# Scores of the third attention: four heads in one run on TensorE, then their four turnings and value products

## The chip, the cores and the metric

The kernel runs on one core of a Trainium2 chip. The metric is the device time of one execution in microseconds (us). The engines are TensorE (PE; its weight loads are listed as PEld), VectorE (DVE), ScalarE (ACT), GpSimd (POOL) and SyncE (SP). Each has its own queue and runs it in the order written; semaphores tie the queues together. Matmul results go to PSUM, which is used as eight banks of 128 x 512 float32.

## The reference, cut to what matters

The program is two blocks in a row. The first is a hybrid layer, run twice (`l` = 0, 1), over 256 "context" rows and 256 "latent" rows, in tiles of 128 rows (tiles 0 and 1 are context, 2 and 3 latent). Each layer has three attentions and a merge. The third attention has 16 query heads of size 64 that share 4 key heads, a window mask and a sink:

```
s_loc = where(mask, q * 64**-0.5 @ kb.T, NEG_INF)
s_ctx = q * 64**-0.5 @ k_ctx.T
p     = softmax(concat([sink, s_ctx, s_loc]))     # float32
o     = p_ctx @ v_ctx + p_loc @ vb
```

Context rows attend to the 256 context rows alone. In layer 0 all four tiles have queries, in layer 1 only the two latent ones. The second block (four mixers) is not touched by the change.

## The kernel before, in words

The four engines' programs are generated by one list of steps. A linear layer is a step "gemm": weights come in by DMA in chunks of 256 rows, ScalarE makes a high part of them (L1265), VectorE the rest (L1774), and TensorE multiplies three times (L872 to L874). `prepare` issues that splitting; inside the third attention it comes once in a layer, on ScalarE ahead of item 32 (layer 0) or 16 (layer 1), on VectorE two items later.

An attention is a list of items, one for each (tile, head). The third has 64 items in layer 0 (0 to 31 on context tiles, with 256 keys; 32 to 63 on latent tiles, with 512 keys) and 32 in layer 1 (all latent). For each item:

- TensorE makes the scores. The head size is 64, so the array of 128 rows is used as two halves of 64 rows, and two heads are made side by side, each in a bank of its own: three steps (L1034, L1037, L1040; high by high, low by high, high by low) of two matmuls each. They are issued at even items only.
- VectorE adds the mask and takes the negative maximum in one instruction, in place in the bank (L2250).
- ScalarE takes the exponential out of the bank into `stage` (L1590), which frees the bank, and the sink's exponential (L1596).
- TensorE turns the probabilities (`turn`, L914, one 128 x 128 transpose per key tile), with item i - 3 (`LAG`).
- VectorE (even items, L2268) or ScalarE (odd items, L1609) copies them to `probs_turned`.
- TensorE multiplies them with the values (L1061), with item i - 5 (`PV_LAG`).
- VectorE scales the output of four heads (L2297, L2299, L2313). It does so after the maximum of item i = 4n + 2, for the group of items that ends with 4n - 1.

The order on VectorE is therefore, for i = 4n to 4n + 3: maximum; maximum, copy; maximum, outputs; maximum, copy. On ScalarE it is exponential and, at every other item, a copy behind it.

Banks: `take` hands out banks in turn from a pool and makes TensorE wait until the last user of the bank has emptied it. Scores use the pool "wide" (banks 0 to 3), the turnings banks 4 and 5, the outputs 6 and 7. Items 0 and 1 are scored earlier, inside the linear layer before, in other banks. So four items' scores fill the pool, and the scores of item i need the banks of item i - 4.

Below, S(i) stands for the scores of items i and i + 1, T(i) for the turning and V(i) for the value product of item i.

Of the kernel before, what the change touches and what calls it, by code (L numbers as in the profile page):

```python
# [28 lines left out]
P = 128  # L29
# [29 lines left out]
FIRST = 2  # L59
# [318 lines left out]
def key_tiles(t):  # L378

    return CTX_TILES if t in CTX_TILES else ALL_TILES  # L380
# [11 lines left out]
def program(nc, dram, out, known):  # L392
    ctx = ExitStack()
    with ctx:
# [7 lines left out]
        def place(name, shape, dt=F32, at=None):  # L402
            size = 4 * int(np.prod(shape[1:]))
            where = top[0] if at is None else at
            if at is None:
                top[0] += (size + 31) // 32 * 32
            return nc.alloc_sbuf_tensor_at(name, shape, dt, offset=where)
# [20 lines left out]
        QH = place("q_high", [P, 8, 512], F32R, at=R)  # L428
        KH = place("k_high", [P, 8, 512], F32R, at=R + K16)
# [78 lines left out]
        banks = [ctx.enter_context(nc.psum_tensor(f"bank{b}", [P, 512], F32)) for b in range(8)]  # L508
# [11 lines left out]
        def probs_at(r, i):  # L520

            return stage(i) if r == 1 else STG[:, 512 * ((i + 4) % 6):512 * ((i + 4) % 6) + 512]
# [7 lines left out]
        def q_low(l, r, h, n, t):  # L530

            if l:
                return QL_LAT[:, h:h + n, P * (t - 2):P * (t - 2) + P]
            return (QL_ACC if r == 1 else QL_X)[:, h:h + n, P * t:P * t + P]

        def k_low(l, r, h, n, cols):

            if r == 2:
                return KL_K[:, h:h + n, cols]
            if l == 0:  # L540
                return KL_X[:, h:h + n, cols]
            return KL_Y[:, h:h + n, cols] if h < 4 else KL_ACC[:, h - 4:h - 4 + n, cols]
# [13 lines left out]

        part_of = {c: n for n, c in enumerate(to_split)}
        summed = {sums.at[m] for u in units for _, sums, m in u.riders}
        first = len(FIRST_LANDING)
        landed_in = list(FIRST_LANDING) + [(c - first) % RAW_SLOTS for c in range(first, len(chunks))]  # L560
# [82 lines left out]
        def items(l, r, qt):  # L643
            return [(t, h) for t in qt for h in range(HEADS[r])]
# [150 lines left out]
        def _(pe):  # L795
# [7 lines left out]
            def take(pool, key):  # L803

                b = POOL[pool][turns[pool] % len(POOL[pool])]
                turns[pool] += 1
                if uses[b]:
                    pe.wait_ge(*S.nth(f"bank{b}_emptied", uses[b]))
                uses[b] += 1
                S.use_bank(key, b, uses[b])  # L810
                return b

            def fills(b):
                return S.up(f"bank{b}_filled")

            def once(event):

                sem, value = event
                if (str(sem), value) not in waited:
                    waited.add((str(sem), value))  # L820
                    pe.wait_ge(sem, value)
# [6 lines left out]
            def gemm(u, turned):  # L828
# [15 lines left out]
                for n, (src, k0, kt, col, width) in enumerate(u.chunks):  # L844
                    while late and late[0][0] <= n:
                        turn(*late.pop(0)[1])
                    if u.more.get("head") and n == 1:
                        l, r, qt = u.more["head"]
                        attend(l, r, qt, 0, FIRST)
# [57 lines left out]
            def turn(key, parts, pool="turn", after=()):  # L907

                for event in after:
                    once(S.at(*event))  # L910
                b = take(pool, key)
                for src, col in parts:
                    p, m = src.shape
                    mm = pe.transpose(banks[b][0:m, col:col + p], src, IDENT[0:p, 0:p])  # L914
                mm.then_inc(*fills(b))
# [81 lines left out]
            def qk_ready(l, r, t, h):  # L997

                q, k = {0: (("uq", l, h // 4), ("ukv", l, h // 2)), 1: (("dq", l, h // 4), ("dk", l, h // 4)),
                        2: (("sq", l, h // 8), ("sk", l))}[r]  # L1000
                once(S.emptied(("turn", q, t)))
                for kt in key_tiles(t):
                    once(S.emptied(("turn", k, kt)))

            def values_ready(l, r, t, h):

                for kt in key_tiles(t):
                    once(S.emptied(({0: ("ukv", l, h // 2), 1: ("dv", l, h // 4), 2: ("sv", l)}[r], kt)))

            def attend_first(l, r, qt):  # L1010
                pass

            def attend(l, r, qt, start=FIRST, stop=None):
                todo = items(l, r, qt)
                width = VALUE[r]
                for i in range(start, stop or len(todo)):
                    if i < len(todo):
                        t, h = todo[i]
                        nk = P * len(key_tiles(t))
                        qk_ready(l, r, t, h)  # L1020
                        if r == 0:
                            b = take("turn4" if i < FIRST else "wide", ("s", l, r, t, h, 0))
                            pe.matmul(banks[b][:, 0:nk], QT[0:MQ, h, P * t:P * t + P], KTT[0:MQ, h, 0:nk],  # L1023
                                      start=True, stop=True).then_inc(*fills(b))
                        elif r == 1 or h % 2 == 0:
                            halves = [(h, 0), (h, 1)] if r == 1 else [(h, 0), (h + 1, 0)]
                            two = [take("turn4" if i < FIRST else "wide", ("s", l, r, t, hh, m)) for hh, m in halves]
                            hq, hk = (h, h) if r == 1 else (h // 2, h // 4)
                            q_high, k_high = QH[:, hq, P * t:P * t + P], KH[:, hk, 0:nk]
                            ql = q_low(l, r, hq, 1, t).rearrange("p a c -> p (a c)")  # L1030
                            kl = k_low(l, r, hk, 1, slice(0, nk)).rearrange("p a c -> p (a c)")
                            for m, b in enumerate(two):
                                a = slice(64 * m, 64 * m + 64)
                                pe.matmul(banks[b][:, 0:nk], q_high[a], k_high[a], start=True, stop=False)  # L1034
                            for m, b in enumerate(two):
                                a = slice(64 * m, 64 * m + 64)
                                pe.matmul(banks[b][:, 0:nk], ql[a], k_high[a], start=False, stop=False)  # L1037
                            for m, b in enumerate(two):
                                a = slice(64 * m, 64 * m + 64)
                                pe.matmul(banks[b][:, 0:nk], q_high[a], kl[a], start=False,  # L1040
                                          stop=True).then_inc(*fills(b))
                    if LAG <= i < len(todo) + LAG:
                        t, h = todo[i - LAG]
                        pe.wait_ge(*S.at("probs", (l, r, t, h)))
                        pr = probs_at(r, i - LAG)
                        turn(("pt", l, r, t, h), [(pr[:, P * n:P * n + P], P * n) for n in range(len(key_tiles(t)))])
                    if i >= PV_LAG:
                        n_item = i - PV_LAG
                        t, h = todo[n_item]
                        g, gn = h // GROUP[r], h % GROUP[r]  # L1050
                        if gn == 0:
                            out_bank[0] = take("out", ("o", l, r, t, g))
                        open_bank = out_bank[0]
                        values_ready(l, r, t, h)
                        pe.wait_ge(*S.emptied(("pt", l, r, t, h)))
                        vcol = h * width if r < 2 else (h // 8) * width
                        kts = key_tiles(t)
                        slot = n_item % PT_SLOTS
                        pt = PTS[:, 512 * slot:512 * slot + 512]
                        for n, kt in enumerate(kts):  # L1060
                            mm = pe.matmul(banks[open_bank][:, width * gn:width * gn + width],  # L1061
                                           pt[:, P * n:P * n + P], V[:, kt, vcol:vcol + width],
                                           start=(n == 0), stop=(n == len(kts) - 1))
                        if gn == GROUP[r] - 1:
                            mm.then_inc(*fills(open_bank))
                            S.same("pt_used", (l, r, n_item), f"bank{open_bank}_filled")
                        else:
                            mm.then_inc(*S.up("pt_used", (l, r, n_item)))
# [1500 lines left out]
```

## Time and profile before

| | |
|---|---|
| time, median of 3 runs | 2450.35 us (2450.02 to 2450.39) |
| the profiled execution: its time | 2452.31 us |
| its span (first to last instruction) | 2450.5 us |
| granted TensorE clock, mean | 0.998 of full speed |
| busy share of the span | PE 98%, PEld 82%, DVE 60%, ACT 49%, POOL 1% |
| third attention, layer 0 | from 726.01 us (S(2)) to 812.02 us (first matmul of the next linear layer) |
| third attention, layer 1 | from 1444.85 us to 1497.58 us |

A row of a timeline gives the start, the duration, the engine, the source line, the operation, what it writes and reads, how many instructions are merged, and in brackets how long the engine sat idle before it and what released it. Matmuls are pipelined: the difference between the starts of two rows is the time that the first costs the engine, and its duration also holds the time until its result is out. A value product of 128 x 128 float32 counts as two instructions.

### The profile page before, as it was taken

To read this page: it belongs to the slowest core of one execution; us is meant where nothing else is said; L and a number is where in the kernel's file an instruction comes from. 1 tells how busy PE (TensorE), PEld (TensorE's weight loads), DVE (VectorE), ACT (ScalarE), POOL (GpSimd) and SP (SyncE) were. 2 spreads that over 40 slices of the span, in tenths; PEclk is the share of its full clock that TensorE was granted. 3 is DMA by queue.
4 is the path that set the end of the run, shared out by engine and by line. 5 is a ranking of instruction groups with operands and counts; after the bars stand their busy time and mean duration, and the time that the engine had idled before them with its cause. 6 is when DMAs were issued, how large, how long until landed. Compare 5 with 4: busy or idle time off the path is not lost.

```text
span 2450.5 us, 33381 instructions
## 1 busy us (share of the span) xinstructions
PE 2401.6 (98%) x12741; PEld 2009.1 (82%) x12741; DVE 1474.1 (60%) x2518; ACT 1190.1 (49%) x2278; POOL 29.9 (1%) x55
## 2 busy tenths in 40 slices
PE   7999999899999999899999999999999999999999
PEld 5978888678888888788887888878888888888887
DVE  3555564876557445565548676665679844566565
ACT  5553223653247332564336455464556554544643
POOL 1100000000000000000000000000000000000000
PEclk9999999999999999999999999999999999999999
DMA  7413553134530222234531623555555561655654
GB/s 253 104 30 104 167 150 86 44 100 133 157 93 10 87 86 78 69 117 130 146 94 41 193 87 92 193 172 185 161 190 185 185 189 40 217 174 163 197 168 133
DMA packets 165007, 318.80 MB, mean 130 GB/s; under 512 B 10470, under 2 KB 22624, under 8 KB 164336
## 3 DMA queue, kind: packets, MB, share of 16 engines
q1 hardware_dynamic: 161552, 303.67, 40.0%
q0 software_dynamic: 3296, 12.98, 1.9%
q8 instruction: 103, 1.69, 0.3%
q14 instruction: 56, 0.46, 0.1%
HBM read 313.46 MB, written 3.15 MB: 129 GB/s over the span
## 4 chain that ended last, share of the span: by engine, by line
PE 90%; DVE 6%; ACT 2%; issue 2%; DMA 0%; SPq 0%; DVEq 0%; ACTq 0%
PE bank L872 24%; PE bank L874 24%; PE bank L873 24%; PE bank L914 7%; PE bank L1061 5%; PE bank L1023 1%; DVE neg_max L2255 1%; DVE w_low_part L1774 1%; PE bank L1034 1%; PE bank L1189 1%; PE bank L1122 1%; PE bank L1148 0%; PE bank L1040 0%; PE bank L946 0%; PE bank L1037 0%
## 5 line engine op out<-in xcount | busy, mean ns | idle before, releaser
L1774 DVE TENSOR_TENSOR w_low_part<-w_raw,w_high_part 128x1024 fp32r<-128x1024 f32 (+3 forms) x544 | 636.8, 1186 | 510.8 <-ACT w_high_part L1265 508.7
L1265 ACT ACTIVATE w_high_part<-w_raw 128x1024 fp32r<-128x1024 f32 (+3 forms) x544 | 552.3, 1031 | 688.5 <-PE bank L874 688.3
L872 PE MATMUL bank<-w_high_part,h_high 128*128 128x512 f32 (+3 forms) x2128 | 817.1, 384 | 5.9 <-DVE w_low_part L1774 2.1
L874 PE MATMUL bank<-w_high_part,h_low 128*128 128x512 f32 (+3 forms) x2128 | 806.9, 379 | 0.0
L873 PE MATMUL bank<-w_low_part,h_high 128*128 128x512 f32 (+3 forms) x2128 | 806.0, 379 | 0.0
L872 PEld LDWEIGHTS bank<-w_high_part,h_high 128*128 128x128 f32 x2128 | 400.1, 188 | 83.5 <-DVE w_low_part L1774 6.0
L874 PEld LDWEIGHTS bank<-w_high_part,h_low 128*128 128x128 f32 x2128 | 399.9, 188 | 74.7
L873 PEld LDWEIGHTS bank<-w_low_part,h_high 128*128 128x128 f32 x2128 | 400.4, 188 | 71.3 <-issue 0.2
L1590 ACT ACTIVATE stage<-bank,neg_max 128x512 f32<-128x512 f32 (+1 forms) x240 | 147.1, 615 | 123.9 <-DVE neg_max L2255 71.1
L1061 PE MATMUL bank<-v,probs_turned 128*128 128x128 f32 x1280 | 173.9, 276 | 0.0
L914 PEld LDWEIGHTS bank<-ident,stage 128*128 128x128 f32 (+1 forms) x1112 | 127.3, 139 | 51.7 <-issue 38.6
L914 PE MATMUL bank<-ident,stage 128*128 128x128 f32 (+1 forms) x1112 | 167.3, 278 | 2.0 <-ACT probs_turned L1715 0.9
L1061 PEld LDWEIGHTS bank<-v,probs_turned 128*128 128x128 f32 x1280 | 158.6, 192 | 0.5
L872 PE MATMUL bank<-w_high_part,y_high 128*128 128x512 f32 x288 | 113.3, 393 | 0.0
L2255 DVE TENSOR_REDUCE neg_max<-bank 128x1 f32<-128x512 f32 (+1 forms) x144 | 81.3, 596 | 52.1 <-PE bank L1023 26.4
L874 PE MATMUL bank<-w_high_part,y_low 128*128 128x512 f32 x288 | 112.1, 389 | 0.0
L873 PE MATMUL bank<-w_low_part,y_high 128*128 128x512 f32 x288 | 112.1, 389 | 0.0
L872 PE MATMUL bank<-w_high_part,wide_high 128*128 128x512 f32 x224 | 88.2, 394 | 1.4 <-DVE w_low_part L1774 1.4
L874 PE MATMUL bank<-w_high_part,wide_low 128*128 128x512 f32 x224 | 87.3, 390 | 0.0
L873 PE MATMUL bank<-w_low_part,wide_high 128*128 128x512 f32 x224 | 87.2, 389 | 0.0
L2250 DVE CUSTOM_DVE_ANT_0 bank<-bank,v,neg_sink 128x512 f32<-128x512 f32 (+1 forms) x96 | 61.8, 668 | 31.7 <-PE bank L1040 31.0
L1609 ACT COPY probs_turned<-bank 128x512 f32<-128x512 f32 (+1 forms) x120 | 60.8, 508 | 27.2 <-PE bank L914 27.2
(315 smaller groups left out, 2491.1 us busy)
## 6 DMA issues: line engine op xcount, KB each, us to landing
w_raw<-in_w_in_dram SPq DMA_DIRECT2D x160, 512.0 KB, 3.6
w_raw<-in_a_w_in_dram SPq DMA_DIRECT2D x96, 512.0 KB, 4.2
w_raw<-in_b_w_in_dram SPq DMA_DIRECT2D x80, 512.0 KB, 4.3
w_raw<-in_w_branch_dram SPq DMA_DIRECT2D x48, 512.0 KB, 3.9
w_raw<-in_w_mod_dram SPq DMA_DIRECT2D x37, 512.0 KB, 4.2
w_raw<-in_a_w_out_dram SPq DMA_DIRECT2D x32, 512.0 KB, 4.6
w_raw<-in_c_w_in_dram SPq DMA_DIRECT2D x32, 512.0 KB, 3.7
w_raw<-in_w_out_dram SPq DMA_DIRECT2D x16, 512.0 KB, 3.9
```

The source lines that it names most:

```text
L872: pe.matmul(o, high, wh, start=(k == 0), stop=False)
L873: pe.matmul(o, high, wl, start=False, stop=False)
L874: mm = pe.matmul(o, low, wh, start=False, stop=(k == u.kt - 1))
L914: mm = pe.transpose(banks[b][0:m, col:col + p], src, IDENT[0:p, 0:p])
L1023: pe.matmul(banks[b][:, 0:nk], QT[0:MQ, h, P * t:P * t + P], KTT[0:MQ, h, 0:nk], start=True, stop=True).then_inc(*fills(b))
L1061: mm = pe.matmul(banks[open_bank][:, width * gn:width * gn + width], pt[:, P * n:P * n + P], V[:, kt, vcol:vcol + width], start=(n == 0), ...
L1265: nc.scalar.activation(WH[:, n % PART_SLOTS, 0:kt, 0:width], raw[:, 0:kt, 0:width], ACT.Copy).then_inc(*S.up("w_high", c))
L1590: nc.scalar.activation(dst[:, 0:nk], ps(key)[:, 0:nk], ACT.Exp, bias=NM[:, i % 8, m:m + 1], scale=-1.0 if r == 2 else 1.0, accum_out=LS[:, ...
L1609: nc.scalar.copy(PTS[:, 512 * slot:512 * slot + nk], ps(key)[:, 0:nk]).then_inc(*S.empties(key))
L1774: v.tensor_tensor(WL[:, s, 0:kt, 0:width], raw[:, 0:kt, 0:width], WH[:, s, 0:kt, 0:width].bitcast(F32), ALU.subtract).then_inc(*S.up("w_lo ...
L2250: mx = v.tensor_tensor_reduce(out=s[:, 0:nk], in0=s[:, 0:nk], in1=WINDOW[:, 1 if t == 3 else 0, 0:nk], scale=-1.0, scalar=NSINK[:, l, h:h ...
L2255: mx = v.tensor_reduce(NM[:, i % 8, m:m + 1], s[:, 0:nk], AX_X, ALU.max, negate=True)
```

## The change

The three steps of a pair's scores move to a function `score_halves`, and `scored_at(r, i)` says which pairs are made at item i. For the second attention (`r == 1`) nothing changes. For the third (`r == 2`) the pairs S(0) and S(2) stay where they were; from i = 4 on, two pairs are made at i = 4, 8, 12, ...: S(i) and S(i + 2). Nothing is made at i + 2.

```
+            def scored_at(r, i):
+
+                if i < FIRST or r == 1 or i == 2:
+                    return (i,) if r == 1 or i % 2 == 0 else ()
+                return (i, i + 2) if i % 4 == 0 else ()
+
+            def score_halves(l, r, i, t, h):
+                nk = P * len(key_tiles(t))
+                qk_ready(l, r, t, h)
+                halves = [(h, 0), (h, 1)] if r == 1 else [(h, 0), (h + 1, 0)]
+                two = [take("turn4" if i < FIRST else "wide", ("s", l, r, t, hh, m)) for hh, m in halves]
...
+                for m, b in enumerate(two):
+                    a = slice(64 * m, 64 * m + 64)
+                    pe.matmul(banks[b][:, 0:nk], q_high[a], k_high[a], start=True, stop=False)
...
-                        elif r == 1 or h % 2 == 0:
-                            halves = [(h, 0), (h, 1)] if r == 1 else [(h, 0), (h + 1, 0)]
...
+                        else:
+                            for n in scored_at(r, i):
+                                score_halves(l, r, n, *todo[n])
                     if LAG <= i < len(todo) + LAG:
```

Only TensorE's order changes; the banks, and what the other engines do in which order, stay. In TensorE's queue, on a context tile of layer 0, this stood before (scores of two heads, then turning and value product twice, then the next scores):

```order
L1034 MATMUL bank<-k_high,q_high 128x256 x2
L1037 MATMUL bank<-k_high,q_low_by_x 128x256 x2
L1040 MATMUL bank<-k_low_by_k,q_high 128x256 x2
L914 MATMUL bank<-ident,stage 128x128 x2
L1061 MATMUL bank<-v,probs_turned 128x128 x2
L914 MATMUL bank<-ident,stage 128x128 x2
L1061 MATMUL bank<-v,probs_turned 128x128 x2
L1034 MATMUL bank<-k_high,q_high 128x256 x2
L1037 MATMUL bank<-k_high,q_low_by_x 128x256 x2
L1040 MATMUL bank<-k_low_by_k,q_high 128x256 x2
```

And this stands there now (scores of four heads, then turning and value product four times; lines 1030, 1033 and 1036 are what 1034, 1037 and 1040 were, 1072 what 1061 was):

```order
L1030 MATMUL bank<-k_high,q_high 128x256 x2
L1033 MATMUL bank<-k_high,q_low_by_x 128x256 x2
L1036 MATMUL bank<-k_low_by_k,q_high 128x256 x2
L1030 MATMUL bank<-k_high,q_high 128x256 x2
L1033 MATMUL bank<-k_high,q_low_by_x 128x256 x2
L1036 MATMUL bank<-k_low_by_k,q_high 128x256 x2
L914 MATMUL bank<-ident,stage 128x128 x2
L1072 MATMUL bank<-v,probs_turned 128x128 x2
L914 MATMUL bank<-ident,stage 128x128 x2
L1072 MATMUL bank<-v,probs_turned 128x128 x2
L914 MATMUL bank<-ident,stage 128x128 x2
L1072 MATMUL bank<-v,probs_turned 128x128 x2
```

The second pair of scores has moved ahead of two turnings and two value products, and so ahead of everything that ScalarE and VectorE did meanwhile for the items whose banks it takes.

VectorE's queue at such a place, the same before and now but for its line numbers (ISA is the masked maximum, whose second row reads its accumulator; the COPY is that of an even item; the three rows from TENSOR_TENSOR on are the outputs):

```order
L2279 COPY probs_turned<-bank 128x256
L2261 ISA bank,neg_max<-bank,v,neg_sink 128x256
L2261 ISA neg_max 128x1
L2308 TENSOR_TENSOR row_inverse<-row_sums,sink_exp 128x4
L2310 RECIPROCAL row_inverse<-row_inverse 128x4
L2324 TENSOR_TENSOR y<-bank,row_inverse 128x256
L2261 ISA bank,neg_max<-bank,v,neg_sink 128x256
L2261 ISA neg_max 128x1
L2279 COPY probs_turned<-bank 128x256
L2261 ISA bank,neg_max<-bank,v,neg_sink 128x256
```

Nothing has moved here: the maxima of items 4n + 2 and 4n + 3 stand behind the copy of item 4n - 2 and around the outputs.

## Rows read from the trace of the kernel before

**Rows 1.** Page, part 4: shares of the chain that ended last, by engine

```profile
PE 90%; DVE 6%; ACT 2%; issue 2%; DMA 0%; SPq 0%; DVEq 0%; ACTq 0%
```

**Rows 2.** Table by stretches (busy us per engine, PEclk, DMA): layer 0's second attention

```profile
444.00:512.00 68.00, 59.60 (x446) 46.13 (x445) 64.78 (x168) 51.83 (x154) 0.53 (x1) 1.00 0.11 40
```

**Rows 3.** Timeline, PE, latent tile of layer 0, one period

```profile
775.06 0.50 PE L1034 MATMUL bank<-k_high,q_high 64*128 64x512 f32 x2
775.40 0.40 PE L1037 MATMUL bank<-k_high,q_low_by_x 64*128 64x512 f32 x2
775.63 0.40 PE L1040 MATMUL bank<-k_low_by_k,q_high 64*128 64x512 f32 x2
775.96 0.66 PE L914 MATMUL bank<-ident,stage 128*128 128x128 f32 x4
776.46 1.06 PE L1061 MATMUL bank<-v,probs_turned 128*128 128x128 f32 x8
777.35 0.60 PE L914 MATMUL bank<-ident,stage 128*128 128x128 f32 x4
777.78 1.06 PE L1061 MATMUL bank<-v,probs_turned 128*128 128x128 f32 x8
778.77 0.50 PE L1034 MATMUL bank<-k_high,q_high 64*128 64x512 f32 x2
```

**Rows 4.** Timeline, PE, context tile of layer 0, one period

```profile
737.23 0.39 PE L1034 MATMUL bank<-k_high,q_high 64*128 64x256 f32 x2
...
737.78 0.44 PE L914 MATMUL bank<-ident,stage 128*128 128x128 f32 x2
...
738.72 0.61 PE L1061 MATMUL bank<-v,probs_turned 128*128 128x128 f32 x4
739.26 0.39 PE L1034 MATMUL bank<-k_high,q_high 64*128 64x256 f32 x2
```

**Rows 5.** Timeline, DVE and ACT, context tile of layer 0

```profile
738.29 0.16 DVE L2297 TENSOR_TENSOR row_inverse<-row_sums,sink_exp 128x4 f32<-128x4 f32 x1
...
739.17 0.49 DVE L2250 CUSTOM_DVE_ANT_0 bank<-bank,v,neg_sink 128x256 f32<-128x256 f32 x1
...
739.58 0.42 DVE L2268 COPY probs_turned<-bank 128x256 f32<-128x256 f32 x1
...
739.81 0.47 ACT L1590 ACTIVATE stage<-bank,neg_max 128x256 f32<-128x256 f32 x1 [0.27 <-DVE neg_max L2250]
739.91 0.49 DVE L2250 CUSTOM_DVE_ANT_0 bank<-bank,v,neg_sink 128x256 f32<-128x256 f32 x1
```

**Rows 6.** Timeline, second attention of layer 0: an exponential and the scores it releases

```profile
446.83 0.47 ACT L1590 ACTIVATE stage<-bank,neg_max 128x256 f32<-128x256 f32 x1
...
447.53 0.39 PE L1034 MATMUL bank<-k_high,q_high 64*128 64x256 f32 x2 [0.52 <-ACT stage L1590]
```

**Rows 7.** Timeline, DVE and ACT, latent tiles of layer 0

```profile
778.05 0.69 DVE L2268 COPY probs_turned<-bank 128x512 f32<-128x512 f32 x1 [0.49 <-PE bank L914]
...
781.33 0.76 DVE L2250 CUSTOM_DVE_ANT_0 bank<-bank,v,neg_sink 128x512 f32<-128x512 f32 x1
...
782.24 0.69 ACT L1590 ACTIVATE stage<-bank,neg_max 128x512 f32<-128x512 f32 x1
```

**Rows 8.** Timeline, layer 0: S(4), exponential of item 3, the wait before T(2)

```profile
726.93 0.38 PE L1034 MATMUL bank<-k_high,q_high 64*128 64x256 f32 x2
...
727.90 0.46 ACT L1590 ACTIVATE stage<-bank,neg_max 128x256 f32<-128x256 f32 x1
...
728.02 0.20 PEld L914 LDWEIGHTS bank<-ident,stage 128*128 128x128 f32 x2 [0.34 <-ACT stage L1590]
```

**Rows 9.** Timeline, layer 0: the part of weights that VectorE splits ahead of item 34

```profile
758.19 1.22 DVE L1774 TENSOR_TENSOR w_low_part<-w_raw,w_high_part 128x1024 fp32r<-128x1024 f32 x1
```

**Rows 10.** Timeline, layer 1: S(4) and the exponential of item 3

```profile
1446.33 0.50 PE L1034 MATMUL bank<-k_high,q_high 64*128 64x512 f32 x2
...
1447.57 0.68 ACT L1590 ACTIVATE stage<-bank,neg_max 128x512 f32<-128x512 f32 x1
```

More of the change, by code:

```diff
@@ L1011, in attend_first @@
                 pass
+            def scored_at(r, i):
[7 more added lines that the diff above has]
+                two = [take("turn4" if i < FIRST else "wide", ("s", l, r, t, hh, m)) for hh, m in halves]
+                hq, hk = (h, h) if r == 1 else (h // 2, h // 4)
+                q_high, k_high = QH[:, hq, P * t:P * t + P], KH[:, hk, 0:nk]
+                ql = q_low(l, r, hq, 1, t).rearrange("p a c -> p (a c)")
+                kl = k_low(l, r, hk, 1, slice(0, nk)).rearrange("p a c -> p (a c)")
+                for m, b in enumerate(two):
+                    a = slice(64 * m, 64 * m + 64)
+                    pe.matmul(banks[b][:, 0:nk], q_high[a], k_high[a], start=True, stop=False)
+                for m, b in enumerate(two):
+                    a = slice(64 * m, 64 * m + 64)
+                    pe.matmul(banks[b][:, 0:nk], ql[a], k_high[a], start=False, stop=False)
+                for m, b in enumerate(two):
+                    a = slice(64 * m, 64 * m + 64)
+                    pe.matmul(banks[b][:, 0:nk], q_high[a], kl[a], start=False, stop=True).then_inc(*fills(b))
             def attend(l, r, qt, start=FIRST, stop=None):
@@ L1024, in attend @@
                                       start=True, stop=True).then_inc(*fills(b))
-                        elif r == 1 or h % 2 == 0:
-                            halves = [(h, 0), (h, 1)] if r == 1 else [(h, 0), (h + 1, 0)]
[L1027 to L1041, printed above, removed]
+                        else:
+                            for n in scored_at(r, i):
+                                score_halves(l, r, n, *todo[n])
                     if LAG <= i < len(todo) + LAG:
```

## The prediction, made before the changed kernel was run

> **What bounds the kernel now.** I read the chain that ended last first: 90% of it is TensorE [rows 1]. So a microsecond that TensorE loses or saves anywhere is a microsecond of the result, unless it waited there. Then the timeline of TensorE in the third attention. On a latent tile the period of two heads is 778.77 - 775.06 = 3.71 us and no row in it names a releaser: TensorE is late by its own work [rows 3]. On a context tile the period is 739.26 - 737.23 = 2.03 us, again without a releaser [rows 4]. Last the timeline of VectorE and ScalarE at the same places, for the length of the path from a turning to a freed score bank [rows 5 to 7]: today nobody waits for that path, and the change puts it in TensorE's way.
>
> **What is saved.** No matmul is added or removed. What goes is the passage between matmuls on 128 rows and the paired ones on 64, once for each joined pair. On a latent tile, from row start to row start [rows 3]: the value product costs 777.35 - 776.46 = 0.89 with a turning behind it and 778.77 - 777.78 = 0.99 with scores behind it (0.10 more); the first score step 0.34 against 0.23 for the second (0.11 more); the third 0.33 (0.10 more); the turning behind the scores 0.50 against 0.43 (0.06 more, by unrounded differences). Sum 0.36 us for a joined pair. If the second pair has to wait for its banks, its first step starts afresh and the 0.11 stays: 0.25. On a context tile the block of scores costs 737.78 - 737.23 = 0.55 [rows 4]; less 0.10 on each side that leaves three steps of 0.12, and the saving is 0.34, or 0.24 with a wait.
>
> The row shows the passage at some 0.1 us on either side. The Trainium skill, page "TensorEngine Tiling (Array Packing)", section "Key Properties", says that a change of the tiling mode drains TensorE; by that rule alone the change could only gain, and the trace agrees as far as the passage goes, though not on what follows from the banks.
>
> Joined pairs: layer 0 has 15 (i = 4 to 60, every fourth), 7 on context and 8 on latent tiles; layer 1 has 7, all latent.
>
> **What is added: waits for banks.** The pair S(4n + 2) now comes right behind S(4n), and takes the banks of items 4n - 2 and 4n - 1. These are free when the exponential of item 4n - 1 is done. Before, T(4n - 3), T(4n - 2) and two value products lay between. What decides when that exponential is done? Take it one group on, the exponential of item 4n + 3, for which S(4n + 6) waits: VectorE has the copy of item 4n - 2 queued ahead of the maximum of item 4n + 2, and the outputs between the maxima of 4n + 2 and 4n + 3. So from the start of T(4n - 2) the path is copy, maximum, outputs, maximum, exponential of item 4n + 3, S(4n + 6). Behind it in TensorE's queue stand all turnings and value products, so a wait there is lost in full.
>
> The path on a context tile: turning to copy 0.48 (a turning is seen 0.10 us after its duration ends, as 778.05 - (777.35 + 0.60) shows [rows 3, 7]; that of a context item not behind scores I estimate at 0.38, the 0.44 of its row less the 0.06 above); copy to maximum 739.91 - 739.58 = 0.33; maximum to outputs 0.41 (739.58 - 739.17, the same to a copy); outputs to maximum 0.88; maximum to exponential 739.81 - 739.17 = 0.64 [rows 5]; exponential to released scores 447.53 - 446.83 = 0.70 [rows 6]. Sum 3.44 us. TensorE's own work between the same two points: three turnings and three value products, 3 x 0.66 + 0.10, then S(4n + 4) with 0.10 + 3 x 0.12: 2.54. (0.66: 739.26 - 738.72 gives 0.54 for the product with its passage, so 0.44 without; 738.72 - 737.78 = 0.94 = 0.28 + 0.44 + 0.22 for turning, product, turning [rows 4].) The wait is 3.44 - 2.54 = 0.90 us for every context group in steady state.
>
> The path on a latent tile: 0.70 to the copy [rows 3, 7], 0.60 copy to maximum (0.69 less the 0.09 that the context row is shorter than its duration), 0.68 (0.76 less 0.08), 0.88, then 782.24 - 781.33 = 0.91 to the exponential and 0.69 + 0.23 = 0.92 to the scores. Sum 4.69. TensorE's work: 3 x (0.43 + 0.89) + 0.10 + 0.34 + 0.23 + 0.23 = 4.86 to 4.89. So the latent groups hide the path, with some 0.2 us to spare.
>
> Group by group, each wait in us:
> - i = 4, layer 0: S(6) is ready at 726.93 + 0.46 = 727.39, the exponential of item 3 starts at 727.90 [rows 8], free at 728.60. Wait 1.2.
> - i = 8: no outputs yet (0.88 shorter), but ScalarE is still behind from the start. Between 0 and 0.9; I take 0.5.
> - i = 12 to 28: five times 0.90, 4.5.
> - i = 32: the path is still a context one, S(32) is latent (0.81 against 0.46): 0.55.
> - i = 36: VectorE has a part of weights to split ahead of the maximum of item 34. It lasts 1.22 and holds the engine 1.13 [rows 9]. Path 0.48 + 0.33 + 1.13 + 0.68 + 0.88 + 0.91 + 0.92 = 5.33; TensorE's work T(30) to V(30), of which only T(32) is latent, and S(36): 2.3 + 0.8 = 3.1. Wait 2.2.
> - i = 40 to 60: none.
> - layer 1, i = 4: ready at 1446.33 + 0.81 = 1447.14; 1447.57 + 0.92 = 1448.49 [rows 10]. Wait 1.35.
> - layer 1, i = 20: the latent path with the 1.13 of the weight part, less the 0.2 to spare: 0.9.
> - layer 1, the rest: none.
> Sum 9.0 + 2.25 = 11.2 us.
>
> That score banks are emptied too late is what the same page of the Trainium skill warns of under "PSUM Bottleneck": tiling makes TensorE faster but not the emptying of PSUM. The page has no figure for it; the sum stands on the rows.
>
> **What goes with it.** The small waits of before at the start of the stage and at the weight part go, since the new ones lie ahead of them: four places, the largest 0.34 [rows 8], together about 1.1 us by my estimate (0 to 1.2).
>
> **The sum.** Saved: 11 latent pairs without a wait x 0.36 = 4.0; 4 latent with a wait x 0.25 = 1.0; 7 context x 0.24 = 1.7; together 6.7. Result: 11.2 - 1.1 - 6.7 = +3.5 us: layer 0 about +3.8, layer 1 about -0.3. The end of the stage adds nothing: the last pairs are scored sooner, and the four banks that the next linear layer takes are free sooner. The profiled execution took 2452.31 us, its span 2450.5; the median without a profile is 2450.35. The sum is of differences inside the span, so I put it on the median: 2453.9 us, slower by 0.14%. The clock should not move: the second attention has TensorE idle in 8 of 68 us (59.60 busy) at a granted clock of 1.00 [rows 2].
>
> Bounds of the unsure terms: the steady context wait is 0.90 give or take 0.15 in its six steps (1.0 us over seven groups); the saving for a joined pair could be nearly nothing if the passage were a price of the wait on a semaphore rather than of the array's shape (+7 us), and is at most 0.36; the wait at i = 36 lies between 1.1 (the 1.13 alone, if the rest were hidden) and 2.4.
>
> **Rivals.**
> First, faster: the second pair doesn't wait to speak of, because ScalarE and VectorE run ahead where four heads lie ready at once. For it: they idle on latent tiles today, and the steady latent groups do hide the path. Against it: VectorE's copy of item 4n - 2 stands in its queue whatever lies ready, so it cannot run ahead. It decides if the context path is below 2.54 us. Then the waits but for the two starts (2.5) vanish: 2.5 - 1.1 - 7.6 = -6.2, 2444.1 us. Half of it (context waits at 0.3) gives about 2449. Chance 0.07 for either.
> Second, slower by more: the latent path isn't hidden. 0.2 us is all it has, and six steps go into it. If it is 0.5 longer than I have it (from a ScalarE that comes late with the copy of item 4n + 1, whose queue is the one I follow least), 11 groups wait 0.3 and lose their 0.11: +4.5 on top of the forecast, 2458.4 us. It decides from a path of 4.9 us on. Chance 0.13.
> Third, the passage isn't saved: the second pair's wait instructions drain the array as a change of shape does. Then a joined pair saves the exit alone, some 0.15: the savings halve, and the result is +7, 2457 us. Chance 0.08.
> The forecast's mechanism as a whole has 0.72, and by its sizes lies between 2451.5 and 2456.
>
> **How the numbers follow.** A run of this kernel tells 0.2% from no change, 4.9 us; that is 2445.4 and 2455.3. Faster by more: the full form of the first rival, 0.04. Slower by more: the second and third rivals nearly whole, 0.19, and the upper edge of the forecast's own sizes, 0.08: 0.27. Within: 0.69. The range that leaves out 2 in 10: 2449.5 to 2457.8, which holds the half form of the first rival, the third in full and the second in part.
>
> **What would show it.** In the profile after: on context tiles a period of four heads of about 4.7 us against 4.06, with one wait of TensorE in it at the first step of the second pair, put down to ScalarE's exponential. On latent tiles 7.05 us against 7.42 and no wait. A wait of over 2 us where the weight part lies on VectorE in layer 0, and one near 0.9 in layer 1. Joined blocks of scores without a wait of 1.6 us (latent). The stage in layer 0 4 us longer, in layer 1 no longer. I am wrong if context tiles have no such waits, or latent tiles do, or if the second pair's first step costs 0.34 where it didn't wait.

## The result and the profile after

The changed kernel takes 2455.41 us (median of 13 runs, 2453.47 to 2456.47); the kernel before, on the same chip, 2450.17 us (13 runs, 2449.65 to 2452.17). The ratio is 1.002, 95% interval 1.0012 to 1.0028: slower by 0.2%, a small loss, but one that the interval sets apart from no change. The forecast was 2453.9, range 2449.5 to 2457.8.

The two profiled executions took 2455.51 and 2452.31 us, their spans are 2453.7 and 2450.5: 3.2 us apart. Measured inside the trace, from S(2) to the first matmul of the next linear layer, the third attention takes:

| | layer 0 | layer 1 | together, against before |
|---|---|---|---|
| before | 726.01 to 812.02: 86.01 us | 1444.85 to 1497.58: 52.73 us | |
| after | 725.81 to 815.62: 89.81 us | 1448.30 to 1500.62: 52.32 us | +3.80 - 0.41 = +3.39 us |

So +3.4 us arise in the stage. The medians are 5.2 apart because some executions of both kernels run about 2 us longer than the others; in the traces of such executions the delay lies ahead of the stage. Of the long kind are nine of the changed kernel's 13 (2454.8 or more), one of before's 13 (2452.17). The last section shows where it arises; one experiment repeats the changed kernel.

The waits of TensorE in the stage, from the list of waits (engine, line, releaser: us in total, times, longest), first of layer 0, then of layer 1:

```profile
PE bank L1030 <- ACT stage L1601: 7.5, 9, 2.1
...
PE bank L1030 <- ACT stage L1601: 2.0, 2, 1.2
```

All are waits for a score bank that an exponential frees; before, the stage had none of this kind. The page's shares of the chain that ended last, for [rows 1], and the table by stretches over layer 0's stage:

```profile
PE 89%; DVE 6%; ACT 2%; issue 2%; DMA 0%; SPq 0%; DVEq 0%; ACTq 0%
```

```profile
725.00:816.00 91.00, 83.51 (x720) 74.48 (x719) 63.96 (x199) 64.31 (x219) 2.12 (x4) 1.00 0.09 27
```

TensorE is busy 83.51 of 91 us, 7.5 less than the stretch, which is the 7.5 of the waits; the granted clock stays at 1.00, its 2.4 GHz level, through them.

Context tile, TensorE, first steps of the scores, for [rows 4]:

```profile
735.60 0.39 PE L1030 MATMUL bank<-k_high,q_high 64*128 64x256 f32 x2
736.97 0.38 PE L1030 MATMUL bank<-k_high,q_high 64*128 64x256 f32 x2 [0.75 <-ACT stage L1601]
...
740.33 0.39 PE L1030 MATMUL bank<-k_high,q_high 64*128 64x256 f32 x2
741.70 0.39 PE L1030 MATMUL bank<-k_high,q_high 64*128 64x256 f32 x2 [0.75 <-ACT stage L1601]
```

Four heads take 740.33 - 735.60 = 4.73 us (before 2 x 2.03). The first pair's three steps cost 0.46, so of the 1.37 to the second pair 0.91 is wait. The list has only 0.75 of it, because it counts idle time from the end of the row ahead: that row (735.94) lasts 0.28, where it costs 0.12 when another follows at once, and the 0.16 between hide as much of the wait. The path that it waits for, from the turning T(10) on, VectorE and ScalarE, for [rows 5]:

```profile
738.24 0.38 PE L914 MATMUL bank<-ident,stage 128*128 128x128 f32 x2
```

```profile
738.73 0.42 DVE L2279 COPY probs_turned<-bank 128x256 f32<-128x256 f32 x1 [1.42 <-PE bank L914]
739.07 0.48 DVE L2261 CUSTOM_DVE_ANT_0 bank<-bank,v,neg_sink 128x256 f32<-128x256 f32 x1
...
739.47 0.16 DVE L2308 TENSOR_TENSOR row_inverse<-row_sums,sink_exp 128x4 f32<-128x4 f32 x1
...
740.34 0.49 DVE L2261 CUSTOM_DVE_ANT_0 bank<-bank,v,neg_sink 128x256 f32<-128x256 f32 x1
```

```profile
740.99 0.47 ACT L1601 ACTIVATE stage<-bank,neg_max 128x256 f32<-128x256 f32 x1 [0.27 <-DVE neg_max L2261]
```

VectorE has sat idle for 1.42 us, although the scores of item 4n + 2 were finished for most of that time: their maximum stands in its queue behind a copy that must wait for its turning. Then copy, maximum, outputs, maximum, exponential, scores: 741.70 - 738.24 = 3.46 us.

Latent tile, TensorE, for [rows 3]:

```profile
773.48 0.50 PE L1030 MATMUL bank<-k_high,q_high 64*128 64x512 f32 x2
773.82 0.39 PE L1033 MATMUL bank<-k_high,q_low_by_x 64*128 64x512 f32 x2
774.04 0.39 PE L1036 MATMUL bank<-k_low_by_k,q_high 64*128 64x512 f32 x2
774.27 0.39 PE L1030 MATMUL bank<-k_high,q_high 64*128 64x512 f32 x2
...
775.04 0.66 PE L914 MATMUL bank<-ident,stage 128*128 128x128 f32 x4
...
780.51 0.50 PE L1030 MATMUL bank<-k_high,q_high 64*128 64x512 f32 x2
```

No releaser; the block of four heads takes 1.56 us, the second pair's first step 0.23 and not 0.34; the period of four heads is 7.03 us against 2 x 3.71.

The waits at the weight part of layer 0 and at the two starts, and that of layer 1's weight part, for [rows 8 to 10]:

```profile
728.40 0.39 PE L1030 MATMUL bank<-k_high,q_high 64*128 64x256 f32 x2 [1.05 <-ACT stage L1601]
...
767.56 0.50 PE L1030 MATMUL bank<-k_high,q_high 64*128 64x512 f32 x2 [2.07 <-ACT stage L1601]
...
1451.92 0.50 PE L1030 MATMUL bank<-k_high,q_high 64*128 64x512 f32 x2 [1.18 <-ACT stage L1601]
...
1480.30 0.50 PE L1030 MATMUL bank<-k_high,q_high 64*128 64x512 f32 x2 [0.78 <-ACT stage L1601]
```

### The profile page after: what moved, and what is told of

It reads as the page before. It is cut to its first block, busy times and chain, and to the rows that moved or that the text cites. A ratio compares the mean times of both kernels' runs of the same rounds, so it can differ in the third digit from the quotient of the medians.

```text
span 2453.7 us, 33381 instructions
## 1 busy us (share of the span) xinstructions
PE 2395.9 (98%) x12741; PEld 2009.6 (82%) x12741; DVE 1473.4 (60%) x2518; ACT 1191.7 (49%) x2278; POOL 29.9 (1%) x55
## 4 chain that ended last, share of the span: by engine, by line
PE 89%; DVE 6%; ACT 2%; issue 2%; DMA 0%; SPq 0%; DVEq 0%; ACTq 0%
PE bank L872 24%; PE bank L874 24%; PE bank L873 24%; PE bank L914 6%; PE bank L1072 4%; PE bank L1048 1%; DVE neg_max L2266 1%; DVE w_low_part L1785 1%; PE bank L1030 1%; ACT stage L1601 1%; PE bank L1200 1%; PE bank L1133 1%; PE bank L1159 0%; PE bank L946 0%; PE bank L1033 0%
## 5 line engine op out<-in xcount | busy, mean ns | idle before, releaser
L2279 DVE COPY probs_turned<-bank 128x512 f32<-128x512 f32 (+1 forms) x72 | 43.1, 598 | 53.0 <-PE bank L914 52.7
```

What stands on the lines that cost most here:

```text
L2279: v.tensor_copy(PTS[:, 512 * slot:512 * slot + nk], ps(key)[:, 0:nk]).then_inc(*S.empties(key))
```

## The experiments

Each was timed in five rounds beside the kernel before. In the table "stage" is the time from S(2) to the next linear layer's first matmul in the kernel's trace, less that of before; before's medians in the three groups of runs were 2450.31 (33 runs), 2450.17 (32) and 2450.04 (18).

| | median us (runs) | ratio, 95% interval | stage, layer 0 | stage, layer 1 |
|---|---|---|---|---|
| latent groups only | 2446.52 (11) | 0.9982 (0.9973 to 0.9991) | -2.20 | -1.86 |
| context groups only | 2454.22 (11) | 1.0014 (1.0005 to 1.0023) | +4.03 | -0.03 |
| all, outputs later | 2450.89 (11) | 1.0001 (0.9992 to 1.001) | +1.19 | -0.63 |
| pairs, outputs later | 2450.7 (11) | 1.0001 (0.9992 to 1.001) | +0.70 | -0.03 |
| the change again | 2453.66 (11) | 1.0016 (1.0007 to 1.0024) | +3.87 | -0.40 |
| all, weight part earlier | 2451.29 (11) | 1.0003 (0.9994 to 1.0012) | +2.73 | -1.47 |
| all, outputs and a copy later | 2448.95 (11) | 0.9993 (0.9984 to 1.0002) | -0.29 | -1.11 |
| gathered | 2445.04 (10) | 0.9979 (0.9969 to 0.9988) | -3.24 | -2.24 |
| gathered again | 2444.51 (10) | 0.9977 (0.9967 to 0.9986) | -3.26 | -2.26 |
| gathered, a copy first | 2444.54 (9) | 0.9976 (0.9967 to 0.9986) | -3.19 | -2.23 |

**Joining only where the path is hidden.** The rule of which pairs are joined is all that is changed against the changed kernel:

```
-                return (i, i + 2) if i % 4 == 0 else ()
+                first = i - i % 4
+                joined = first >= 40 if l == 0 else first >= 8 and first != 20
+                if not joined:
+                    return (i,)
+                return (i, i + 2) if i == first else ()
```

> Pairs are joined only where the path from a turning to the freed score bank is hidden: latent tiles, without the first group and without the groups that a weight part delays (layer 0: i = 40 to 60, layer 1: i = 8, 12, 16, 24, 28; 11 joined pairs). My theory (a saved passage of 0.36 us a pair, and no wait on latent tiles): 11 x 0.36 = 4.0 us faster than before, 2446.2 us, no new wait of TensorE in the profile. Rival (joining costs time by itself, or scatter and clock take the gain): 2450 us or more.

Measured 2446.52. TensorE has no wait for an exponential in either layer. The stage gives the price of the passage by itself: 2.20 us for six joined pairs and 1.86 for five, 0.37 us each (0.36 was worked out). With the Trainium skill's rule that a change of the tiling mode drains TensorE ("TensorEngine Tiling (Array Packing)", section "Key Properties") the trace agrees, in that leaving out the change back and forth saves these 0.37 us; the page gives no figure.

**Joining only on context tiles.** The same edit with `joined = l == 0 and 4 <= first < 32`.

> The other half: pairs are joined only on the context tiles of layer 0 (i = 4 to 28, 7 joined pairs). My theory (each steady group waits some 0.75 to 0.9 us for the exponential, saves 0.24): slower than before by 3 to 4 us, about 2453.7 us, with 7 waits of TensorE at the first step of the second pair. Rival (the latent tiles or the weight parts are what costs): within 1 us of before.

Measured 2454.22. The list of waits in layer 0 (of its score line, L1036 in this kernel):

```profile
PE bank L1036 <- ACT stage L1607: 5.0, 7, 1.0
```

Seven joined pairs, seven waits, and the whole stage 4.03 us longer. The two runs part the change in a gain on latent tiles and a loss on context tiles, of the same size: the stages are 4.06 us shorter and 4.00 longer. What they don't contain is the latent groups at i = 32 and 36 of layer 0 and i = 4 and 20 of layer 1, which wait for the start, the context path or the weight part. By the starts of their rows in the changed kernel's trace these four groups take 0.12, 1.98, 0.75 and 0.68 us more than before. As the other two parts cancel, the +3.39 us of the whole change is in the sum what these four lose.

**Taking the outputs out of the path.** VectorE's outputs move from behind the maximum of item 4n + 2 to behind that of item 4n + 3, with the change in force:

```
+                after = PV_LAG + 3 if r == 2 else PV_LAG + 2
...
-                    if i >= PV_LAG + 2 and last_in_group(i - PV_LAG - 2):
+                    if i >= after and last_in_group(i - after):
```

> The changed kernel (all pairs joined), and VectorE makes the outputs of a group one item later: behind the maximum of item 4n + 3 and the copy, not between the maxima of 4n + 2 and 4n + 3. That takes 0.88 us out of the path. My theory: the steady context waits go from 0.75 to about 0, the wait at i = 36 from 2.1 to 1.2, the one at i = 20 of layer 1 to 0, the two at the start stay: faster than the changed kernel by 6 to 8 us, about 2446.5 us at the level of the shortest executions, faster than before. Rival (the waits come from ScalarE's own queue): the waits stay, 2454 us or more.

Measured 2450.89: my expectation was missed by 4.4 us. The context wait fell from 0.75 to 0.38 idle and no further. ScalarE's timeline, and the scores that waited:

```profile
742.12 0.47 ACT L1601 ACTIVATE stage<-bank,neg_max 128x256 f32<-128x256 f32 x1 [0.50 <-DVE neg_max L2262]
...
742.77 0.36 ACT L1620 COPY probs_turned<-bank 128x256 f32<-128x256 f32 x1
743.02 0.48 ACT L1601 ACTIVATE stage<-bank,neg_max 128x256 f32<-128x256 f32 x1
```

```profile
743.74 0.39 PE L1030 MATMUL bank<-k_high,q_high 64*128 64x256 f32 x2 [0.38 <-ACT stage L1601]
```

The last exponential no longer waits for its maximum (no releaser at 743.02); it is late by ScalarE's own queue, the exponential before it and the copy between. The wait at i = 36 fell to 1.49 and that of layer 1 at i = 20 to 0.57, where I had written 1.2 and 0. I had taken 0.88 us out of VectorE's part and not asked what was late next.

**The same move without joining**, as a control (`joined = False`).

> Control: the kernel before (pairs not joined) with the outputs one item later as well. My theory: TensorE doesn't wait for that path there, so nothing moves, 2450.2 us within 0.5. Rival (the later outputs are worth something by themselves): 1 us or more faster.

Measured 2450.7, nothing that can be told from before; by the trace the move alone costs 0.7 us in layer 0, where four heads on a context tile take 4.18 us and not 4.06. So it is worth something only where it shortens a path that TensorE waits for.

**The changed kernel once more**, to see whether 2455.4 or 2453.5 is its time.

> The changed kernel once more, to tell where its median of +5.2 us comes from when its profile has the stage only 3.4 us longer. In all kernels so far some executions are about 2 us longer than the rest, and the two profiles of before and after differ from the later ones within the first 30 us of the program. Theory: that is chance, the same in every kernel; then the shortest executions are again near 2453.6, 3.5 above those of before, and the share of long ones is like that of the others (about one in three). Rival: the changed kernel has the long form more often by itself; then its median is 2455.4 again.

Measured 2453.66: six of the 11 lie between 2452.97 and 2453.66, five between 2454.95 and 2456.16. The stage is +3.47 us, as in the first trace, so what the change does to it is settled. That the share of long executions is chance, as I wrote, is not borne out: over both groups of runs it is 14 of 24, where before has 23 of 96 (2451.5 or more). Before's own share varies from 1 of 13 to 12 of 33 between the groups of runs.

**The weight part out of the path.** VectorE splits it behind the maximum of item 33 (17 in layer 1), ahead of the copy for whose turning it would be idle anyway, and no longer behind that copy:

```
-                    if i == len(todo) // 2 + 2:
+                    if r != 2 and i == len(todo) // 2 + 2:
...
+                    if r == 2 and i == len(todo) // 2 + 1:
+                        prepare(by_key[("z", l, r, 0)].pfirst + PART_SLOTS)
```

> The changed kernel, with VectorE's weight part one step earlier: behind the maximum of item 33 (layer 0) or 17 (layer 1) and ahead of the copy, where VectorE waits for a turning anyway. My theory: the wait at i = 36 of layer 0 falls from 2.07 to about 1.0, the one at i = 20 of layer 1 from 0.78 to 0; 2 us faster than the changed kernel, about 2451.7 us at the level of the shortest executions. Rival (the splitting isn't on the path; the passage from context to latent tiles is what costs): no change.

Measured 2451.29. Waits of layer 0, and the wait at i = 36:

```profile
PE bank L1030 <- ACT stage L1601: 6.4, 9, 1.0
```

```profile
764.61 0.50 PE L1030 MATMUL bank<-k_high,q_high 64*128 64x512 f32 x2 [0.98 <-ACT stage L1601]
```

2.07 fell by 1.09, nearly the 1.13 for which the part holds VectorE, and the wait of layer 1 at i = 20 is gone. One instruction in each layer, on the wrong side of a copy in VectorE's queue, had cost 2.1 us of both layers' stages together.

**Outputs and a copy later.** As above with the outputs later, and on ScalarE the copy of item 4n - 1 behind both exponentials instead of between them:

```
+                    if r == 2 and 8 <= i < len(todo):
+                        if i % 4 == 0:
+                            turned(l, r, todo, i - 3)
+                        if i % 4 == 3:
+                            turned(l, r, todo, i - 4)
```

> The kernel with the outputs later had 0.38 us of wait left in each steady context group, with ScalarE's copy of item 4n - 1 between the exponentials of 4n + 2 and 4n + 3. Here that copy comes behind both as well. Path by the trace's rows: 0.49 + 0.34 + 0.64 + 0.66 + 0.72 = 2.85 us against 2.54 us of TensorE's work. Theory: the wait falls to about 0.13 idle, 1.5 us faster than with the outputs later alone, 2449.4 us. Rival (something else of ScalarE or PSUM holds it): still 0.38, 2450.9.

Measured 2448.95. Waits of layer 0:

```profile
PE bank L1030 <- ACT stage L1601: 2.2, 3, 1.0
PE bank L914 <- ACT probs_turned L1625: 0.7, 3, 0.3
```

The copy was the next link: 4.7 us of waits for score banks in layer 0 became 2.2. Of the three that are left one is at i = 4, one small at i = 8, one at the weight part. But the three short waits of the second line are new, and a context group still takes 4.18 us: 4.36 with the outputs alone later, 4.06 before, and the same 4.18 in the control without joining. From one period of TensorE:

```profile
744.27 0.39 PE L1030 MATMUL bank<-k_high,q_high 64*128 64x256 f32 x2
...
746.29 0.61 PE L1072 MATMUL bank<-v,probs_turned 128*128 128x128 f32 x4
747.00 0.41 PE L914 MATMUL bank<-ident,stage 128*128 128x128 f32 x2
...
748.45 0.39 PE L1030 MATMUL bank<-k_high,q_high 64*128 64x256 f32 x2
```

The value product at 746.29 costs 0.71 us here and 0.45 where nothing holds the turning behind it. That turning starts 0.51 behind a copy of ScalarE (746.49) that empties a bank of the turnings; the last experiment moves this copy.

**Gathered.** All groups from i = 8 are joined, and both other engines work in fours: VectorE four maxima, copy, outputs, copy; ScalarE exponential, copy, three exponentials, copy; the weight parts stand at the end of a latent group. The core of VectorE's side:

```
+                    if 8 <= i < n_all:
+                        if i % 4:
+                            continue
+                        for m in range(4):
+                            maximum(i + m)
+                        copy(i - 2)
+                        output(i - 5)
+                        copy(i)
```

> All that follows from the theory at once: pairs are joined from i = 8 on; VectorE makes the four maxima in a row, then copy, outputs, copy; ScalarE one exponential, a copy, three exponentials, a copy; both weight parts stand at the end of a latent group. Theory: no wait of TensorE beyond those of the kernel before at the start; 6 context pairs x 0.34 + 14 latent x 0.36 = 7.1, and 0.2 for the weight part: 2442.9 us, faster than both kernels. Rival (four heads at once need a fifth bank whatever the order): waits of 0.3 or more in each context group, 2445 us or more.

Measured 2445.04, and 2444.51 when run again: faster than both kernels, though 2 us short of what I expected. TensorE waits for no exponential any more. The rival of my expectation, waits of 0.3 in each context group, had the right time, but it is out by its mechanism. A context group takes 3.91 us, where a period of 4.06 less the 0.34 for the passage gives 3.72; over five groups that is 0.95 of the 1.7 us by which layer 0 saved less than expected (3.24 of 4.92), and the groups at i = 8 and i = 32 are the rest. Its TensorE and ScalarE rows (second trace):

```profile
738.13 0.61 PE L1078 MATMUL bank<-v,probs_turned 128*128 128x128 f32 x4
738.58 0.38 PE L914 MATMUL bank<-ident,stage 128*128 128x128 f32 x2
738.79 0.61 PE L1078 MATMUL bank<-v,probs_turned 128*128 128x128 f32 x4
739.40 0.41 PE L914 MATMUL bank<-ident,stage 128*128 128x128 f32 x2
...
740.85 0.39 PE L1036 MATMUL bank<-k_high,q_high 64*128 64x256 f32 x2
...
741.32 0.28 PE L1036 MATMUL bank<-k_high,q_high 64*128 64x256 f32 x2
```

```profile
738.25 0.47 ACT L1607 ACTIVATE stage<-bank,neg_max 128x256 f32<-128x256 f32 x1 [0.71 <-DVE neg_max L2269]
...
738.90 0.36 ACT L1633 COPY probs_turned<-bank 128x256 f32<-128x256 f32 x1
```

From the value product at 738.79 to the next turning are 0.61 us, from the one at 738.13 only 0.45. No wait is listed, yet 0.16 is lost. The third turning takes the bank of the first, which ScalarE's copy at 738.90 empties, behind an exponential that itself waited 0.71 us. (The value product lasts 0.61 and costs 0.45, so its row covers the wait; a wait of up to 0.16 us never shows in such a list.)

**That copy first.** On ScalarE, for i = 12 to 28 of layer 0, the copy of item 4n - 3 goes ahead of the exponential of item 4n:

```
-                        if i % 4 == 0:
+                        ahead = lambda n: l == 0 and 12 <= n < 32
+                        if i % 4 == 0 and not ahead(i):
...
+                            if ahead(i + 1):
+                                turned(l, r, todo, i - 2)
```

> The gathered version, with one copy moved on ScalarE: on the context tiles of layer 0 (i = 12 to 28) the copy of item 4n - 3 now stands ahead of the exponential of item 4n instead of behind it. In the gathered version TensorE stops at 739.25 to 739.86 (0.61 us where a value product and its passage cost 0.445), right after that copy (739.36, 0.36 us) has freed the bank that the third turning takes; and ScalarE is idle 0.71 us before the exponential. My theory is that this bank is the cause: then the 0.61 shrinks to about 0.45, the period of four context heads falls from 3.91 to some 3.80 us (the exponentials come 0.1 later, which the second pair of scores just feels), and five groups give 0.5 us: about 2444.5. The rival is that the gap is one of items or of VectorE's copy of item 4n - 2: then the gap stays, and with the exponentials later the period grows to 4.0 and the time to 2445.5.

> The gathered version once more, unchanged, beside the one with the copy moved: 2445.0, within 0.5 us, and the same period of 3.91 us on context tiles.

Measured 2444.54 and 2444.51: no difference. TensorE's rows with the copy first:

```profile
736.94 0.39 PE L1036 MATMUL bank<-k_high,q_high 64*128 64x256 f32 x2
...
739.04 0.61 PE L1078 MATMUL bank<-v,probs_turned 128*128 128x128 f32 x4
739.49 0.38 PE L914 MATMUL bank<-ident,stage 128*128 128x128 f32 x2
...
740.91 0.39 PE L1036 MATMUL bank<-k_high,q_high 64*128 64x256 f32 x2
...
741.53 0.38 PE L1036 MATMUL bank<-k_high,q_high 64*128 64x256 f32 x2
```

```profile
740.82 0.48 ACT L1607 ACTIVATE stage<-bank,neg_max 128x256 f32<-128x256 f32 x1
```

The gap is gone (0.45), so the bank was its cause. But the second pair of scores now starts 0.62 and not 0.47 us behind the first. It follows the last exponential ahead of it by 741.53 - 740.82 = 0.71, the 0.70 from an exponential to released scores of [rows 6]: the exponentials come later and the loss has moved to their banks. The second pair's own three steps, which now start afresh, cost 0.10 more on top (0.54 against 0.44). The first group alone, i = 12, took 3.72. The period is 740.91 - 736.94 = 3.97 us, not the 3.80 that I expected. I had priced the later exponentials at 0.1 for "just feels"; they took back all that the copy gave.

## Why the prediction was right, step by step

- *Savings.* 0.36 us for a joined latent pair: 0.37 in the run with latent groups only. The third rival (the passage isn't saved) is out: the second pair's first step costs 0.23.
- *The context path.* 3.44 us worked out, 3.46 measured; the wait 0.90 worked out, 0.91 measured in each of the five steady groups, and the period 4.73 against 4.7.
- *The latent path.* Hidden, as worked out, so the second rival is out: period 7.03 to 7.06 against 7.05, no wait from i = 40 on.
- *The single waits*, from row starts, with what was forecast: i = 4 1.21 (1.2), i = 8 0.39 (0.5), i = 32 0.56 (0.55), i = 36 767.56 - 764.53 - 0.81 = 2.22 (2.2); layer 1 1.33 (1.35) and 1480.30 - 1478.55 - 0.81 = 0.94 (0.9). Sum 11.2 us, as forecast.
- *The first rival* (no waits, faster) is out: VectorE sat idle 1.42 us ahead of the copy that was said to hold it.
- *The small waits that go*: 1.1 by estimate. No run shows this term by itself; 11.2 of waits less 6.7 of savings leaves 4.5, against 3.39 measured, so 1.1 is also what is left for it.
- *The sum.* Worked out +3.5 (layer 0 +3.8, layer 1 -0.3); the stage shows +3.39 (+3.80, -0.41).
- *Why the banks are late.* Not because TensorE's work got shorter by tiling: tiling and matmuls are the same in both kernels, and what made the banks late is the order in TensorE's queue.
- *What was off*: the time itself, 2453.9 forecast and 2455.41 measured. I put the +3.5 on before's median, which is one of short executions, while most of the changed kernel's first 13 were long. The profiled execution of before, at 2452.31, was one of the long kind and stood 2 us above its median; I noted it and did not ask why. Long against long (2452.31 and 2455.51) the difference is 3.2 us, short against short (about 2450.0 and 2453.5) 3.5. That the measured 2455.41 still fell within the range owes something to the range's width: the mechanism gives 2453.9.

In my own experiments I did worse than in the prediction, and always in the same way: with the outputs later, and again with the copy first, I removed the link that ended last and booked the whole wait as gain, without working out what was late next.

## What to carry to other kernels

Before work is moved up in one engine's queue past work of its own, walk the path through the other engines that frees what the moved work needs, and compare it with what still stands between on the first engine; here it was longer by 0.9 us on short tiles and shorter by 0.2 on long ones, so the same edit lost 4 us on one kind and gained 4 on the other, and the groups at the seams, where the queues hold something extra or are still behind, decided the result. If one engine's order is gathered in fours, look at the orders of the engines that feed it as well: all three gathered gave 5.5 us by the stage, the first alone lost 3.4. Not all of the difference is the gathering: that version also leaves i = 4 in pairs and moves the weight part, which alone is worth 2.1, and joining only the eleven hidden pairs gave 4.1 with no other engine touched. Where a link of a tight loop is taken out, the gain ends at the second latest link.

## What the hardware showed that was not expected

The times of a kernel can fall into two groups about 2 us apart: before lay near 2450.0 (73 of 96) or near 2452.2. The difference arises long before the third attention, in the first 30 us. The table by stretches (busy us of PE, PEld, DVE, ACT and POOL with counts of instructions, clock, DMA share, GB/s) over 20 to 30 us, of before (2452.31 us), after (2455.51) and the repeat of after (2453.66):

```profile
20.00:30.00 10.00, 9.51 (x67) 4.60 (x66) 1.05 (x5) 2.07 (x5) 0.00 (x0) 1.00 1.06 388
```

```profile
20.00:30.00 10.00, 9.51 (x66) 4.37 (x65) 1.27 (x5) 2.30 (x5) 0.00 (x0) 1.00 1.06 387
```

```profile
20.00:30.00 10.00, 8.19 (x77) 3.76 (x76) 2.56 (x7) 2.94 (x6) 0.00 (x0) 1.00 1.05 386
```

In the longer executions TensorE gets through fewer matmuls in the same 10 us (its busy share is 9.51 in the three long traces, the third that of the outputs and a copy later, and 8.19 or 8.20 in the nine others), at the same granted clock of 1.00 and the same DMA rate, and S(2) of layer 0 starts at 725.8 to 726.1 us against 723.8 to 724.3. The first matmuls there, of the modulation weights, take longer each (mean of one, ns):

```profile
L899 PE MATMUL bank<-w_raw,cond 128*2 128x256 f32 x24 | 2.7, 624 | 0.0
```

```profile
L899 PE MATMUL bank<-w_raw,cond 128*2 128x256 f32 x32 | 2.1, 378 | 0.0
```

(before, then the repeat of after). The share of the long ones differs between kernels, from 14 of 24 for the changed one to none of 11 for the changed one with the outputs later or with the weight part earlier, and they differ only behind this place. What decides it was not tried and stays open; so it stays open too whether the changed kernel's median owes its last 1.5 us to the change.
